# Retention scores with both query parts in one 256-column operand

## What is computed

```python
def step(state, qkv):
    qi, ki, vi = qkv
    scores = jnp.einsum('bhnd,bhmd->bhnm', qi, ki) * decay_in
    o = (jnp.einsum('bhnm,bhmv->bhnv', scores, vi)
         + jnp.einsum('bhnd,bhdv->bhnv', qi, state) * decay_q[:, :, None])
    state = (state * decay_chunk[:, None, None]
             + jnp.einsum('bhmd,bhmv->bhdv', ki * decay_k[:, :, None], vi))
    return state, o
```

## Time and profile before

| | |
|---|---|
| median of 3 runs | 2048.53 us (2047.41 to 2049.98) |
| the profiled execution | 2047.54 us |
| its span, first to last instruction | 2045.9 us |
| PE busy | 1999.9 us (98%) |
| DVE, ACT, POOL busy | 1407.6, 904.0, 232.8 us |
| GpSimd between the steps of the retention | two low parts of some 1.3 us and one of some 2.4 us a step in heads 1 to 3 |

### The profile page before, as it was taken

How to read it: one execution, slowest core, us unless ns; L and a number is a source line. 1 busy time by engine, 2 the same in 40 slices (tenths; PEclk the granted TensorE clock), 3 DMA queues, 4 the chain that set the end, 5 groups by cost and what they waited for, 6 DMA issues and landing times.

```text
span 2045.9 us, 26772 instructions
## 1 busy us (share of the span) xinstructions
PE 1999.9 (98%) x10100; PEld 1700.8 (83%) x10100; DVE 1407.6 (69%) x1714; ACT 904.0 (44%) x1154; POOL 232.8 (11%) x187
## 2 busy tenths in 40 slices
PE   7999999999999999999799999999999999999998
PEld 6888888888889999887688888898788888888887
DVE  6976776776644444612877877837988788776766
ACT  6443353343445555401444444335554444443335
POOL 0000010010000000011145545300000000000000
PEclk9999999999999999999999999999999999999999
DMA  5333444444554342436333343741322222246523
GB/s 205 120 137 130 164 161 168 164 168 160 185 177 175 143 155 103 145 123 204 90 119 98 97 126 110 267 146 62 103 82 82 82 82 86 78 155 241 211 97 135
DMA packets 188682, 283.11 MB, mean 138 GB/s; under 512 B 9792, under 2 KB 132032, under 8 KB 188352
## 3 DMA queue, kind: packets, MB, share of 16 engines
q1 hardware_dynamic: 168304, 204.52, 30.1%
q0 software_dynamic: 20304, 77.60, 9.8%
HBM read 198.20 MB, written 83.89 MB: 138 GB/s over the span
## 4 chain that ended last, share of the span: by engine, by line
PE 89%; DVE 7%; issue 1%; ACT 1%; DMA 1%; SPq 0%; DVEq 0%; ACTq 0%
PE ps L309 29%; PE ps L311 29%; PE ps L310 29%; DVE wx L1863 1%; PE ps L1059 1%; DVE ost L1811 1%; DMA raw<-w_ret_o 0%; PE ps L370 0%; DVE stage L1968 0%; DVE tt L1825 0%; PE ps L1090 0%; PE ps L1012 0%; DMA raw<-w_in 0%; DVE gt L2368 0%; DVE vt L2368 0%
## 5 line engine op out<-in xcount | busy, mean ns | idle before, releaser
L1284 ACT ACTIVATE wx<-raw 128x1024 fp32r<-128x1024 f32 (+1 forms) x152 | 137.3, 905 | 270.7 <-DVE raw L1839 148.5
L309 PE MATMUL ps<-xs,wx 128*128 128x512 f32 x612 | 239.0, 390 | 2.1 <-DVE xs L2267 1.6
L310 PE MATMUL ps<-xs,wx 128*128 128x512 f32 x612 | 238.2, 389 | 0.0
L311 PE MATMUL ps<-xs,wx 128*128 128x512 f32 x612 | 238.1, 389 | 0.0
L292 DVE TENSOR_TENSOR ws<-raw,ws 128x2048 fp32r<-128x2048 f32 x32 | 73.3, 2290 | 179.3 <-ACT ws L288 179.3
L1863 DVE TENSOR_TENSOR wx<-raw,wx 128x1024 fp32r<-128x1024 f32 (+1 forms) x152 | 156.1, 1028 | 32.2 <-ACT wx L1284 32.2
L309 PE MATMUL ps<-sc,wx 128*128 128x512 f32 x448 | 174.7, 390 | 1.2 <-ACT ub L1316 1.2
L310 PE MATMUL ps<-sc,wx 128*128 128x512 f32 x448 | 174.3, 389 | 0.0
L311 PE MATMUL ps<-sc,wx 128*128 128x512 f32 x448 | 174.3, 389 | 0.0
L311 PE MATMUL ps<-ws,actv 128*128 128x256 f32 x512 | 144.9, 283 | 0.0
L310 PE MATMUL ps<-ws,actv 128*128 128x256 f32 x512 | 144.9, 283 | 0.0
(11 more groups left out here) (267 smaller groups left out, 4934.6 us busy)
## 6 DMA issues: line engine op xcount, KB each, us to landing
raw<-w_in SPq DMA_DIRECT2D x80, 512.0 KB, 5.3
scr<-ost POOLq DMA_DIRECT2D x32, 1024.0 KB, 5.4
raw<-w_up SPq DMA_DIRECT2D x44, 512.0 KB, 3.9
tq<-w_down SPq DMA_DIRECT2D x88, 128.0 KB, 3.1
scr_t<-tq POOLq DMA_DIRECT2D x22, 512.0 KB, 3.2
scr_h<-vt POOLq DMA_DIRECT2D x11, 1024.0 KB, 4.3
scr_v<-ost POOLq DMA_DIRECT2D x8, 1024.0 KB, 4.6
qkv<-scr SPq DMA_DIRECT2D x64, 128.0 KB, 2.9
```

Of the source, the lines that this page charges most:

```text
L309: pe.matmul(out, w(HI), x(HI), start=first, stop=False, skip_group_check=True)
L310: pe.matmul(out, w(HI), x(LO), start=False, stop=False, skip_group_check=True)
L311: return pe.matmul(out, w(LO), x(HI), start=False, stop=last, skip_group_check=True)
L1284: act.activation(dst, src, ACT.Copy).then_inc(sem["f_hi"], 1)
```

## The change

The high and low part of q lie in `qkvs` at a fixed distance, so a matmul can stream both as one operand of 256 columns: 128 columns of the high part, then 128 of the low part. With the high part of k as weights, high x high lands in the first 128 columns of a PSUM region of 256, and high x low in the second 128. The third product, low part of k with the high part of q, is added into the first 128. Per step these are four matmuls, two of 256 columns and two of 128. The two slots take columns 0 to 255 and 256 to 511 of the same bank.

VectorE then reads the 256 columns with a reduction over pairs that lie 128 columns apart, and writes the sums to `sc`. After a wait on that (`sc_mk`, which now counts two a step) it multiplies `sc` by constant and mask, in place. ScalarE and TensorE wait for the second of the two counts.

```diff
                 pe.wait_ge(sem["qsp"], r + 1)
                 if not (isinstance(r, int) and r < 1):
-                    pe.wait_ge(sem["sc_mk"], r)
+                    pe.wait_ge(sem["sc_mk"], r * 2)
+                both, sum_at = ps[:, 0, 2 * slot * P:2 * (slot + 1) * P], ps[:, 0, 2 * slot * P:(2 * slot + 1) * P]
                 for m in range(2):
-                    last = mm3(pe, ps[:, 0, slot * P:(slot + 1) * P], k_(slot, m), q_(slot, m), m == 0, m == 1)
+                    pe.matmul(both.rearrange("p (a c) -> p a c", a=2), k_(slot, m)(HI), qkvs[:, slot, :, m * P:(m + 1) * P],
+                              start=m == 0, stop=False, skip_group_check=True)
+                    last = pe.matmul(sum_at, k_(slot, m)(LO), q_(slot, m)(HI), start=False, stop=m == 1,
+                                     skip_group_check=True)
                 last.then_inc(sem["sc_ps"], 1)
...
-                act.wait_ge(sem["sc_mk"], r + 1)
+                act.wait_ge(sem["sc_mk"], r * 2 + 2)
...
-                dve.scalar_tensor_tensor(out=sc[:, slot, :], in0=ps[:, 0, slot * P:(slot + 1) * P],
+                dve.tensor_reduce(out=sc[:, slot, :], in_=ps[:, 0, 2 * slot * P:2 * (slot + 1) * P].rearrange(
+                    "p (a c) -> p c a", a=2), axis=mybir.AxisListType.X, op=ALU.add).then_inc(sem["sc_mk"], 1)
+                dve.wait_ge(sem["sc_mk"], r * 2 + 1)
+                dve.scalar_tensor_tensor(out=sc[:, slot, :], in0=sc[:, slot, :],
                                          scalar=con[:, ds(h + CON["unchunk"], 1)], in1=mask[:, :], op0=ALU.mult,
                                          op1=ALU.mult).then_inc(sem["sc_mk"], 1)
```

## The result

The changed kernel takes 2057.55 us in the median of 5 runs (2056.63 to 2058.07); the kernel before, on the same chip in the same comparison, 2048.53 (2046.81 to 2050.93). The ratio is 1.004, with a 95% interval of 1.0027 to 1.0053: slower by 9.0 us. The forecast was 2057.1.

What follows compares the result with a forecast made beforehand. TensorE was taken to bound the kernel, with 89% of the chain. Heads 1 to 3 at 2.5 us each (7.4) and head 0 at 1.2 gave +8.6 us on the median: 2057.1, range 2051 to 2063.

Steps and rivals of the forecast that it cites:

- E + 1.22: Heads 1 to 3: TensorE's state update starts 1.22 us after GpSimd's operation ends; S marks a step's first score matmul.
- TensorE's saving: Score matmuls of each step: four take 0.36 to 0.46 us for 0.62, saving 0.22, at most 7 us over all.
- VectorE's plain extra: Where VectorE is late without GpSimd: reduction, wait and masking in place of one operation cost 0.4 us more.
- Step 1: Second step of heads 1 to 3: update moves from 1125.03 for 1124.65 before, +0.38 us, swallowing TensorE's saving.
- Step 4: In heads 1 to 3: the masking waits about 2 us behind GpSimd's delayed operation, update +1.55 us.
- Step 6: In heads 1 to 3: wait for GpSimd +0.70, slower first matmul +0.11, lateness of the weight split 0.3: +1.1 us.
- Step 2: In heads 1 to 3: update +0.21 us behind GpSimd, first matmul after a wait +0.11, in all +0.32.
- step 3: In heads 1 to 3: an earlier TensorE wait puts GpSimd 0.3 us ahead, so no wait and -0.22.
- Case (c): Half the waits, as where VectorE comes first to the lock: +2 to +4 us, about 2051.5; chance 0.09.
- Rival (b): The wait in step 4 of heads 1 to 3 drops TensorE's clock, 1.7 us each: +5.1, 2062.2; chance 0.22.
- Head 0: First head: GpSimd in the way only in step 0; +1.0 there, +0.4 in step 6, -0.22 in step 7: 1.2 us.
- Step 0: In head 0: masking waits behind GpSimd's operation, update at 966.33 for 965.35, +1.0 us.

Runs made afterwards that it cites:

- e1: Changed kernel with the mask read from a PSUM copy, plus a wait for ScalarE's high part of k: 2050.67 us, ratio 1.0011 to the kernel before.
- e7: Changed kernel with GpSimd's state operation cut to 32 of 512 columns of each half: 2048.67 us, ratio 0.9996 to the kernel before.
- e3: Changed kernel's four matmuls, but one masking straight from PSUM of the first 128 columns, leaving out one product: 2043.62 us, ratio 0.9973 to the kernel before.
- e5: As e4, but the new form only in steps 0, 2, 3, 5, 7 of heads 1 to 3 and step 7 of head 0: 2044.93 us.
- e2: Kernel before with its six matmuls, but VectorE copies the scores to SBUF and masks there: 2061.04 us, ratio 1.0063 to the kernel before.
- the second execution: The changed kernel unaltered, run and profiled once more in a later batch: 2057.0 us, ratio 1.0039 to the kernel before.
- e4: As e1 in heads 1 to 3, with head 0 in the form of the kernel before: 2046.72 us, ratio 0.999 to the kernel before.
- e8: Kernel before with GpSimd's state operation cut as in e7, as its control: 2049.15 us, ratio 0.9999 to the kernel before.

## Why the prediction was right

**The mechanism.** The masking waits to the end E of GpSimd's operation, and TensorE's update follows at E + 1.22. That held to 0.02 us: in step 4 of head 2, E = S + 4.19 and the update at S + 5.40; in step 1, 1.88 and 3.10; in step 6, 3.31 and 4.53. e1 takes the masking's second SBUF input away and e7 the long GpSimd operation; with either the wait goes, and with it the loss of heads 1 to 3.

The Trainium skill (SBUF — State Buffer, section Who interferes with whom) describes this as a lock that an instruction holds for its whole length. The 1.20 us for one element beside GpSimd, and the 0.35 of e1 with one input in PSUM, agree with it.

**TensorE's saving.** The four matmuls take 0.41 us, within 0.36 to 0.46. These rows are head 2, step 4 of the changed kernel, and answer to the earlier trace rows:

```profile
1155.89 0.28 PE L1008 MATMUL ps<-qkvs 128*128 128x256 f32 x1
...
1156.30 0.40 PE L1016 MATMUL ps<-ident,qkv 128*128 128x128 f32 x2
```

A step bound by TensorE saves 0.19 to 0.27 for the 0.22 taken. In heads 1 to 3 of the changed kernel these are the steps 0, 2, 5 and 7. Over all steps the saving could not have passed the 7 us of the forecast, and e3 measured 5.7.

**VectorE's plain extra.** The reduction took 0.42 for 0.41. The masking starts 0.45 after it begins (0.46 by the terms) and takes 0.35 when free; I had put 0.28. The next operation starts 0.26 later in step 4 of e7, not the 0.2 of the sum. So the extra of 0.4 where VectorE is late without GpSimd came at +0.46 (e7, step 4).

**Step 1** came at +0.39 for +0.38. **Step 4** at +1.3 for +1.55: GpSimd's operation ran at S + 0.65 rather than S + 0.87 against TensorE, and by E + 1.22 just that is missing. The masking there took 1.42, not "about 2". **Step 6** at +1.21, +1.28 and +0.98 for +1.1; the assumed lateness of the split is there, with E at S + 3.31 for S + 2.86.

**Steps 2 and 3 were wrong.** Step 2 was forecast at +0.32 and came at -0.26. The working took GpSimd's operation to stand where it stood before, at S. In the changed kernel it starts at S - 1.0 and ends at S + 1.39, and the masking, which starts at S + 1.26, isn't held up. The failed step is the fixed place: the forecast left out that VectorE's coefficient operation and GpSimd's low part of v could change places a step earlier. A wait of TensorE, which I had noted for step 3 as putting GpSimd ahead, isn't what did it: in e5 TensorE waits no longer than before in step 1, and GpSimd stands at S - 1.0 all the same. And behind the 1.3 us that step 4 grew by, GpSimd's operation in step 5 moved by 0.07 only (S - 0.65 for S - 0.58), since VectorE, on which it hangs, is late too. In step 3 GpSimd stands at S - 0.33 as before and not 0.3 further ahead. So the masking waits there (0.94), the update follows at E + 1.21 = S + 3.26 where it could have come at S + 3.13, and the -0.22 became 0. The two terms were off by -0.58 and +0.23, some 1 us over three heads, the cheaper way. Case (c) had VectorE coming first to the lock as a reason for fewer waits; it held in one step of a head.

**Rival (b) came in part.** The clock fell after step 4 in one head of three, for 1.6 us where 1.7 was put. The idling ahead of it was 2.1 us, not 2.9. I had argued against it that TensorE is busy right before and after; it is, and it was no protection. e2 had it in two heads. What tells head 3 from heads 1 and 2, whose waits are as long (2.1 us), no run shows.

**Head 0** came to +2.0 for +1.2, in the second execution to +1.5. Step 0, forecast at +1.0, grew by 1.85 and in the second execution by 0.87. In the first the masking takes 1.06 and the update comes after a wait of 1.78 us, at S + 2.69; the matmuls behind it then follow each other every 0.43 us in place of 0.23, at the lower clock. In the second the wait is 2.02 us and the clock stays full behind it. Head 0's length isn't steady enough to judge its sum: in e4 and e8, which leave head 0 as it was before, it still comes out 0.5 and 1.3 us longer than in the trace of before.

So the total, 8.6 forecast and 9.0 measured, is closer than its terms. Heads 1 to 3 come to 7.4 in the profile, as forecast, but steps 2 to 4 came out some 1.8 us cheaper and the clock in head 3 was 1.6 dearer; that these cancel is luck. The 0.8 that head 0 is dearer by lies within its own variation. By the signs named ahead: the updates of steps 4 moved by 1.3 against S, the wait for the low part of k more than doubled (6.9 to 16.4), in steps 1, 4 and 6 and not in 2, and the masking reaches 1.44. The mean of the masking is 0.71, below the 0.8 to 1.2 put for it, since steps 0 and 2 don't wait.

## What to carry to other kernels

Before an operation is added to VectorE, look where its inputs lie and what GpSimd runs at that time: with two inputs in SBUF it can wait for the whole of GpSimd's operation, here for up to 1.1 us beyond its own 0.35, and with one in PSUM it didn't (e1). A saving on TensorE is worth having in the steps that TensorE bounds, and only there: in all steps the edit cost 9.0 us, and only in the right ones, with the mask read from PSUM, it gained 3.4 (e5). Read the step table, not the sum, to find them.

## What the runs showed of the hardware

- The order of two starts 0.01 us apart decided between 0.16 and 1.20 us for a one-element operation, and moved the next GpSimd operation by 1.0 us against TensorE. A sum made in the clock of before has no row for that.
- A single wait of 2.1 us in a stretch in which TensorE is otherwise busy throughout was followed by some 3 us at 1.2 GHz in one of three equal places, in the same one in both profiled executions.
